# A hybrid diffusion layer with 16 experts: in experts 1 to 13 the next rows are turned later on VectorE and the ranking counts move behind the evacuations; one block of work is moved ahead in three other places

## The chip, the cores and the metric

The kernel runs on one core of one Trainium2 chip. The metric is the device time of one execution in microseconds (us); lower is better. The program is written by hand for each engine: TensorE (PE), VectorE (DVE), ScalarE (ACT), GpSimd (POOL) and SyncE (SP, which only issues DMA transfers). Each engine works through its own list in order, and semaphores tie the lists together.

## The reference, cut to what matters

One layer of a hybrid trunk, on 128 context tokens and 1024 latent tokens of width 1024. First a token mixer (a gated linear memory "mLSTM", a state space scan, and windowed attention, all from one projection), then a mixture of 16 experts in which every expert picks its tokens:

```python
def ec_moe(h, router_w, w1, w3, w2):
    xt = h.reshape(B * T, D)
    cap = EC_FACTOR * (B * T) // N_EXPERTS          # 128 latent, 16 context tokens
    aff = jax.nn.softmax((xt @ router_w).astype(jnp.float32), axis=-1)
    gate_vals, idx = lax.top_k(aff.T, cap)
    xe = xt[idx]
    hid = jax.nn.silu(jnp.einsum('ecd,edf->ecf', xe, w1)) * jnp.einsum('ecd,edf->ecf', xe, w3)
    ye = jnp.einsum('ecf,efd->ecd', hid, w2) * gate_vals[..., None]
    y = jnp.zeros_like(xt).at[idx.reshape(-1)].add(ye.reshape(-1, D).astype(xt.dtype))
```

Ahead of both halves each token row is normalised and modulated by six vectors `mod = silu(c) @ ada_w + ada_b`, whose products are cut into 24 slabs of 256 columns.

## The kernel before

All products are float32. The order of the work is written out by hand; two tables set where small pieces go.

**mLSTM stage.** 18 units (2 directions x 9 chunks of 128 tokens) run one after the other on PE: `m_scores(u + 1)`, `m_state(u)`, `m_values(u)`, `m_update(u)`. Between them stand blocks of the input projection ("T" blocks: 8 products of 128x384) and transposes ("X"), which the table `M_FILL` spreads over 36 slots. `M_FILL[0]` is called between `m_scores(0)` and `m_scores(1)`, and `m_scores(1)` waits for the weights of unit 0 (`mP`), which DVE makes from the scores of unit 0.

**Attention stage.** 27 units; `late_product(m)` for the last 16 slabs of `ada_w` stands behind the units of the list `MOD_UNITS`, and `late_pick(m)` one unit later.

**Expert stage.** For each of 16 experts PE makes `hidden(e)`: 8 blocks `fb`, each a product with w1 and one with w3 (8 matmuls each, 128x144), into PSUM banks 0/1 and 2/3; then `second(e)`: 8 blocks `db` of 8 matmuls with w2, by turns into bank 4 (even) and bank 5 (odd). I call the start of `hidden` N and the start of `second` T. ACT makes the silu of the w1 product, DVE multiplies it with the w3 product (the "mult", 8 per expert). ACT evacuates bank 4, DVE bank 5. Block `db` may only start when block `db - 2` is evacuated:

```python
pe.wait_ge(e_yA if db % 2 == 0 else e_yD, e * 4 + (db // 2 + 1))
```

In the same time the next expert is got ready:
- DVE `rank_begin(e+2)` and `rank_count(e+2, ...)` find each token's rank for expert e+2: 8 counts of 128x1024 in four pairs, and a cast of the ranks behind the second and the fourth pair, which sets `ranks_set`.
- POOL (`expert_rows`) then, strictly in order: four list scatters behind the first cast, four behind the second, the scatter of y of the expert before (four quarters, then a wait until they have landed), and the gather of the rows of expert e+1 (four quarters, `xq`).
- DVE `x_turned(e+1)` waits for that gather, turns the rows with four 32x32 stream transposes and sets `ex_full`. ACT and DVE (`x_evac`) each wait for `ex_full`, then scale half of the turned rows into `xeT`.
- On ACT `x_evac` stands ahead of the evacuation of `db` 0; in its list are 8 silus, `x_evac`, four evacuations, and the scaling of y.
- At the end of the expert DVE turns y (`yq`, 4 transposes) and scales it.

Experts 1 to 13 are a loop on ACT, DVE and POOL (the Fori of `expert(e, False)`); PE and SP are written out. Experts 0 and 14 turn the next rows on PE (`x_turn_latent`, 8 transposes into banks 6 and 7).

Of the kernel before, what the change touches and what calls it, by code (L numbers as in the profile page):

```python
# [22 lines left out]
KD = D // P  # L23
# [103 lines left out]
def hybrid_layer(nc, x_prompt, x_sample, cacheT_k, cache_v, state_c, state_n, state_sT, vec_rows, small_row, ada_w,  # L127
# [4 lines left out]
    groups, n_gate, n_early, n_first = plan_groups()  # L132
# [5 lines left out]
    def spread(first, last, slots):  # L138

        cost = [{"C": 0, "X": 4, "H": 3, "T": 52, "R": 34}[groups[n][0]] for n in range(first, last)]  # L140
        out, done, n = [], 0, first
        for t in range(slots):
            mine = []
            while n < last and (t == slots - 1 or done + cost[n - first] / 2 <= sum(cost) * (t + 1) / slots):
                mine.append(n)
                done += cost[n - first]
                n += 1
            out.append(mine)
        return out

    M_FILL = spread(n_early, n_first, 34) + [[], []]
    BRIDGE = [n_first, n_first + 1]
    base, S_FILL = spread(n_first + 2, len(groups), 33) + [[], [], []], []
    merged = groups[:n_first + 2]
# [46 lines left out]
    with ExitStack() as ctx:  # L201
# [236 lines left out]
        e_h1, e_h3, e_sil, e_hid = sem("e_h1_full"), sem("e_h3_full"), sem("e_silu_done"), sem("e_hidden_done")  # L438
        xgl_in, ex_full, ex_act, ex_dve = (sem(n) for n in ("e_gather_latent", "e_x_full", "e_x_act", "e_x_dve"))
# [75 lines left out]
            d, ch = UNITS[u]  # L515
            return (0 if ch == 0 else 2) + d

        MOD_UNITS = [1, 2, 5, 6, 8, 9, 11, 12, 13, 14, 17, 18, 19, 20, 22, 23]


        AU = [(hp, -1) for hp in range(HN // 2)] + [(hp, t) for hp in range(HN // 2) for t in range(NL)]
# [470 lines left out]
        def _(act):  # L992
# [401 lines left out]
            def silu_hidden(e, tiles={}):  # L1394

                for fb in range(KD):
                    act.wait_ge(e_h1, e * KD + (fb + 1))
                    act.wait_ge(e_hid, e * KD + (fb + 1))
                    nc.scalar.activation(sil[:, fb % 2, :], bk[fb % 2][:, 0:SLOTS], ACT.Silu).then_inc(e_sil, 1)  # L1399
                    for i in tiles.get(fb, ()):  # L1400
                        tile_square(i)

            def y_blocks(e, tiles=()):

                for db in range(0, KD, 2):
                    act.wait_ge(e_yt, e * KD + (db + 1))
                    nc.scalar.activation(yT[:, db, :], bk[4][:, 0:P], ACT.Copy, scale=modcol[:, 40 + db, 1:2])  # L1407
                    nc.scalar.activation(ycT[:, db, bass.ds(e, 1), :].rearrange("p a s -> p (a s)"), bk[4][:, P:SLOTS], ACT.Copy,
                                         scale=modcol[:, 40 + db, 0:1]).then_inc(e_yA, 1)
                    for i in tiles[db // 2:db // 2 + 1]:  # L1410
                        tile_square(i)

            def y_evac(e, rows=False):

                y_blocks(e)
                act.wait_ge(e_ty, e + 1)
                act.wait_ge(gcur_set, e + 1)
                if rows:
                    act.wait_ge(e_free, e + 1)
                    nc.scalar.activation(by_block(ye)[:, 0:4], block_rows(bk[6]), ACT.Copy, scale=gcur[:, 0:1]).then_inc(e_yeA, 1)  # L1420
                    return
                for a in range(2):
                    ins = nc.scalar.activation(yq[:, a, :], yq[:, a, :], ACT.Copy, scale=gcur[:, a:a + 1])
                ins.then_inc(e_yeA, 1)

            def one_expert(e, x_rows=False, y_rows=False):

                silu_hidden(e)
                act.wait_ge(ex_full, e + 2)
                act.wait_ge(e_h3, e * KD + KD)  # L1430
                x_evac(x_psum if x_rows else xturn)
                y_evac(e, y_rows)
# [26 lines left out]
        def _(pe):  # L1459
# [356 lines left out]
            a_scores(1)  # L1816
            pe.wait_ge(cache_in, 32)
            pe.wait_ge(sY, NU)
            for a in range(NA):
                if a + 2 < NA:  # L1820
                    a_scores(a + 2)
                if a >= 1:
                    a_values(a - 1)
                if a - 1 in MOD_UNITS:
                    late_pick(8 + MOD_UNITS.index(a - 1))
                a_turned(a)
                if a in LATE_UNITS:
                    y_late(LATE_UNITS.index(a))
                if a in MOD_UNITS:
                    late_product(8 + MOD_UNITS.index(a))  # L1830
                if a == MOD_UNITS[3] + 1:
                    pe.wait_ge(modT_done, 12)
                    nc.tensor.transpose(bk[7][0:16, 384:512], modcol[:, 16:24, :].rearrange("p a b -> p (a b)"), ident[:])\
                        .then_inc(g1_full, 1)
# [193 lines left out]

            for e in range(NE - 1):
                hidden(e)  # L2030
                if e in (0, NE - 2):
                    pe.wait_ge(xgl_in, fetched(e + 1))
                    pe.wait_ge(e_yeA, e + 1)
                    pe.wait_ge(e_yeD, e + 1)
                    x_turn_latent(0, KD)
                pe.wait_ge(e_hid, e * KD + (KD + 1))
                second(e)
                if e == 0:
                    pe.wait_ge(e_yA, e * 4 + 4)
                    pe.wait_ge(e_yD, e * 4 + 4)  # L2040
                    y_turned(e)
# [28 lines left out]
        def _(dve):  # L2070
# [609 lines left out]
            def expert(e, is_first, x_rows=False, is_last=False):  # L2680

                dve.wait_ge(e_yeA, e + 1)
                dve.wait_ge(e_yeD, e + 1)
                v.tensor_copy(gcur, lists[:, bass.ds(e * 8, 8)].rearrange("p (a w) -> p a w", w=2)[:, :, 1]).then_inc(gcur_set, 1)
                if is_first:
                    rank_begin(1)
                for fb in range(KD):
                    if is_first and fb < 3:
                        rank_count(1, ((0, 1, 2), (3, 4, 5), (6, 7))[fb])
                    dve.wait_ge(e_sil, e * KD + (fb + 1))  # L2690
                    dve.wait_ge(e_h3, e * KD + (fb + 1))
                    v.tensor_tensor(hid[:, fb, :], sil[:, fb % 2, :], bk[2 + fb % 2][:, 0:SLOTS], ALU.mult)\  # L2692
                        .then_inc(e_hid, 1)
                    if fb == KD - 2 and not (is_last or x_rows):
                        x_turned(e + 1)
                if is_last:
                    dve.wait_ge(vecs_in, 16 * 4)
                    tile_scales(1, 2)
                else:
                    dve.wait_ge(ex_full, e + 2)  # L2700
                    x_evac(e + 1, x_psum if x_rows else xturn)
                    rank_begin(e + 2)
                for db in range(1, KD, 2):
                    if not is_last:
                        rank_count(e + 2, (db - 1, db))
                    dve.wait_ge(e_yt, e * KD + (db + 1))
                    v.tensor_scalar(yT[:, db, :], bk[5][:, 0:P], modcol[:, 40 + db, 1:2], None, ALU.mult)
                    v.tensor_scalar(ycT[:, db, bass.ds(e, 1), :].rearrange("p a s -> p (a s)"), bk[5][:, P:SLOTS],
                                    modcol[:, 40 + db, 0:1], None, ALU.mult).then_inc(e_yD, 1)
                    if is_last and db < KD - 2:  # L2710
                        tile_scales(db + 2, db + 3)
                    if is_last and db == KD - 3:
                        dve.wait_ge(xgl_in, fetched(NE - 1) + 16)
                        dve.wait_ge(e_free, NE)
                        dve.wait_ge(gcur_set, NE)
                        last_rows(0)
                if is_last:
                    last_rows(1)
                    return
                dve.wait_ge(e_free, e + 1)  # L2720
                dve.wait_ge(gcur_set, e + 1)
                if is_first:
                    dve.wait_ge(e_ty, e + 1)
                    v.tensor_scalar(by_block(ye)[:, 4:KD], block_rows(bk[7]), gcur[:, 0:1], None, ALU.mult).then_inc(e_yeD, 1)
                    return
                dve.wait_ge(e_yA, e * 4 + 5)
                dve.wait_ge(e_yD, e * 4 + 5)
                for a in range(4):
                    ins = v.transpose(yq[:, a, :].rearrange("p (j k) -> p k j", k=KD), yT[:, :, 32 * a:32 * a + 32])
                ins.then_inc(e_ty, 1)  # L2730
                dve.wait_ge(e_ty, e + 1)
                for a in range(2, 4):
                    ins = v.tensor_scalar(yq[:, a, :], yq[:, a, :], gcur[:, a:a + 1], None, ALU.mult)
                ins.then_inc(e_yeD, 1)
# [71 lines left out]
```

## Time and profile before

| what | us |
|---|---|
| three runs | 1626.65, 1628.55, 1628.59 (median 1628.55) |
| the profiled execution, its time | 1628.24 |
| its span in the profile | 1626.5 |
| PE busy in it | 1579.8 |
| expert stage: first `hidden` starts, last block ends | 849.4, 1613.9 |

The profile follows one execution. "Busy" is the time in which an engine has an instruction in work; an idle time is put down to what ended it ("<-"). A float32 matmul shows as two records, so `second` of one expert (64 matmuls) has 128 records, and `hidden` 256. A line number is that of `kernel.py`.

### The profile page before, as it was taken

What the parts mean: (1) busy time and instruction counts of PE and PEld (TensorE: products, weight loads), DVE (VectorE), ACT (ScalarE), POOL (GpSimd) and SP (SyncE); (2) the same over time, 40 slices, a digit from 0 to 9 for tenths busy, and PEclk for the clock granted to TensorE, in tenths of its full rate; (3) what the DMA queues carried; (4) which work ended last, traced back from release to release, by engine and by line L of the source; (5) the groups of instructions that cost most, each with busy time, mean ns of one, the idle gap of its engine ahead of it and who ended that gap; (6) DMA issues with size and microseconds to landing.
All of it is one profiled execution on the core that took longest, in us unless ns stands there. A gap on an engine that the chain in (4) does not pass through costs nothing. (4 is left out here: it accounts for less than half of the span.)

```text
span 1626.5 us, 28425 instructions
## 1 busy us (share of the span) xinstructions
PE 1579.8 (97%) x11188; PEld 1377.2 (85%) x11188; DVE 714.6 (44%) x1867; ACT 387.3 (24%) x970; POOL 474.2 (29%) x556
## 2 busy tenths in 40 slices
PE   6999999999999899999988999999999999999997
PEld 5866876666668767788878999999999999999997
DVE  4001046776565844222363345444334454443344
ACT  5210113341222476411131111111111111111114
POOL 3000000015232643121202343433344343334432
PEclk9999999999999999999999999999999999999999
DMA  8302211132312476423259999999999999999985
GB/s 348 113 11 88 79 37 58 38 126 30 60 29 90 130 248 206 154 69 101 91 200 353 304 287 303 321 315 296 286 297 306 287 321 330 298 286 287 316 263 228
DMA packets 190733, 324.85 MB, mean 200 GB/s; under 512 B 36110, under 2 KB 76167, under 8 KB 185625
## 3 DMA queue, kind: packets, MB, share of 16 engines
q1 hardware_dynamic: 151017, 282.70, 50.7%
q0 software_dynamic: 15520, 17.45, 5.5%
q10 hardware_dynamic: 24080, 23.02, 5.1%
q8 instruction: 89, 1.46, 0.4%
q14 instruction: 27, 0.22, 0.0%
HBM read 294.42 MB, written 25.51 MB: 197 GB/s over the span
## 5 line engine op out<-in xcount | busy, mean ns | idle before, releaser
L1990 PE MATMUL psum<-arena 128*128 128x144 f32 x4096 | 504.8, 286 | 2.0 <-DVE arena L2632 1.7
L1990 PEld LDWEIGHTS psum<-arena 128*128 128x128 f32 x4096 | 502.9, 190 | 2.4 <-ACT arena L1367 1.9
L2002 PE MATMUL psum<-arena 128*128 128x144 f32 x2048 | 254.4, 286 | 0.0
L2002 PEld LDWEIGHTS psum<-arena 128*128 128x128 f32 x2048 | 252.8, 190 | 0.0
L1573 PE MATMUL psum<-arena 128*128 128x384 f32 x720 | 243.1, 493 | 0.0
L905 POOL DMA_INDIRECT expert_list<-gt x128 | 130.1, 1016 | 320.1 <-DVE gt L2662 286.5
L1573 PEld LDWEIGHTS psum<-arena 128*128 128x128 f32 x720 | 134.6, 191 | 90.2 <-issue 3.1
L2692 DVE TENSOR_TENSOR arena<-gt,psum 128x144 f32<-128x144 f32 x128 | 38.8, 303 | 360.3 <-PE psum L1990 310.3
L2514 DVE SCALAR_TENSOR_TENSOR arena<-arena,gt 128x1024 f32<-128x1024 f32 x128 | 159.1, 1280 | 0.5 <-DMA arena<-affinity_rows 0.5
L1576 PE MATMUL psum<-arena 128*128 128x256 f32 (+2 forms) x784 | 146.4, 346 | 0.0
L1576 PEld LDWEIGHTS psum<-arena 128*128 128x128 f32 x784 | 129.4, 190 | 15.5 <-issue 1.7
L1879 PE MATMUL psum<-arena 128*128 128x256 f32 x576 | 128.4, 381 | 0.7 <-DVE arena L2435 0.7
L1399 ACT ACTIVATE gt<-psum 128x144 f32<-128x144 f32 x128 | 37.0, 289 | 380.9 <-PE psum L1990 374.1
L1879 PEld LDWEIGHTS psum<-arena 128*128 128x128 f32 x576 | 107.9, 190 | 17.1 <-issue 2.1
L786 POOL TENSOR_TENSOR arena<-arena,gt 128x260 f32<-128x260 f32 x18 | 11.4, 635 | 307.6 <-DVE arena L2153 194.7
L955 POOL DMA_INDIRECT moe_latent<-arena,gt x56 | 88.2, 1576 | 24.2 <-issue 18.5
L1407 ACT ACTIVATE arena<-psum,modcol 128x128 f32<-128x128 f32 x64 | 23.5, 367 | 165.2 <-PE psum L2002 165.2
L939 POOL DMA_INDIRECT arena<-h_latent,gt x52 | 51.2, 984 | 23.8 <-issue 13.7
L827 POOL TENSOR_TENSOR arena<-Hst,gt 64x192 f32<-64x192 f32 x36 | 24.2, 673 | 112.0 <-DVE Hst L2351 110.6
L2417 DVE CUSTOM_DVE_ANT_0 gt<-psum,arena 128x512 f32<-128x512 f32 x48 | 31.3, 689 | 57.8 <-PE psum L1754 57.8
L888 POOL TENSOR_TENSOR arena<-arena 128x1024 f32<-128x1024 f32 x8 | 18.8, 2349 | 92.5 <-DVE arena L2471 92.5
L854 POOL TENSOR_TENSOR arena<-arena 128x384 f32<-128x384 f32 x30 | 30.0, 1017 | 47.2 <-DVE arena L2417 47.2
(379 smaller groups left out, 1632.1 us busy)
## 6 DMA issues: line engine op xcount, KB each, us to landing
arena<-in_exp_w SPq DMA_DIRECT2D x96, 2048.0 KB, 15.0
arena<-in_ada_w SPq DMA_DIRECT2D x24, 1024.0 KB, 7.0
arena<-in_w_in SPq DMA_DIRECT2D x11, 1024.0 KB, 4.9
arena<-in_x_sample SPq DMA_DIRECT2D x16, 512.0 KB, 4.4
arena<-affinity_rows SPq DMA_DIRECT2D x16, 512.0 KB
arena<-m_decay_rows ACTq DMA_DIRECT2D x36, 128.0 KB, 3.3
arena<-decay_rows ACTq DMA_DIRECT2D x24, 192.0 KB, 3.5
out<-arena SPq DMA_DIRECT2D x9, 512.0 KB, 2.6
```

Source lines behind the costliest of these rows:

```text
L905: pool.indirect_dma_start(out=list_d, out_offset=bass.IndirectOffsetOnAxis(ap=rank_i[:, c:c + 1].bitcast(U32), axis=0), in_=pair[:, c, :], ...
L939: pool.indirect_dma_start(out=xq[:, a, :], out_offset=None, in_=h2q_d, in_offset=bass.IndirectOffsetOnAxis(ap=icur[:, a:a + 1].bitcast(U32 ...
L955: pool.indirect_dma_start(out=accq_d, out_offset=bass.IndirectOffsetOnAxis(ap=icur[:, 4 + a:5 + a].bitcast(U32), axis=0), in_=yq[:, a, :], ...
L1399: nc.scalar.activation(sil[:, fb % 2, :], bk[fb % 2][:, 0:SLOTS], ACT.Silu).then_inc(e_sil, 1)
L1573: ins = mm(ps[0:cols, 0:384], ring[:, s % RING, k, col:col + cols], hT[:, k, i * 384:i * 384 + 384], start=(k == 0), stop=(k == KD - 1))
L1576: ins = mm(ps[:, 0:cols], hT[:, k, i * P:i * P + P], ring[:, s % RING, k, col:col + cols], start=(k == 0), stop=(k == KD - 1))
L1879: ins = mm(out, mixed(k, i), ring[:, (WOUT + j) % RING, k, :], start=(k == 0), stop=(k == KD - 1))
L1990: ins = mm(bank[:, 0:SLOTS], w[:, k, col], xeT[:, k, :], start=(k == 0), stop=(k == KD - 1))
L2002: ins = mm(bk[4 + db % 2][:, 0:SLOTS], wslot[4 + db // 4][:, k, (db % 4) * P:(db % 4) * P + P], hid[:, k, :], start=(k == 0), stop=(k == K ...
L2417: v.tensor_tensor_reduce(sc_sb[:, a % 3, e, :], ps, tab[:, table_of(a) % 2, e, :], -1.0, 3e38, ALU.add, ALU.min, accum_out=col).then_inc(a ...
L2514: return v.scalar_tensor_tensor(scratch, row, col, before[:, o:o + row.shape[1]], ALU.subtract, ALU.is_gt, accum_out=out)
L2692: v.tensor_tensor(hid[:, fb, :], sil[:, fb % 2, :], bk[2 + fb % 2][:, 0:SLOTS], ALU.mult)\
```

## The change

Five edits: (1) `M_FILL[0]` gets the first T block of the table, and the rest is spread over the slots again; (2) the first late product goes ahead of the unit loop; (3) in expert 0 PE does blocks 0 to 3 of `second` before it turns the rows of expert 1, ACT evacuates blocks 0 and 2 before its `x_evac`, and DVE blocks 1 and 3 before its own; (4) in experts 1 to 13 `x_turned(e+1)` moves behind the mult of `fb` 7 (before: behind that of `fb` 6); (5) in experts 1 to 14 each pair of counts stands behind the evacuation of its block (before: ahead of it). ACT's list in experts 1 to 13, and all of POOL's and SP's, stay.

```diff
-    M_FILL = spread(n_early, n_first, 34) + [[], []]
+    M_FILL = spread(n_early + 1, n_first, 34) + [[], []]
+    M_FILL[0] = [n_early] + M_FILL[0]
...
-        MOD_UNITS = [1, 2, 5, 6, 8, 9, 11, 12, 13, 14, 17, 18, 19, 20, 22, 23]
+        MOD_UNITS = [0, 2, 5, 6, 8, 9, 11, 12, 13, 14, 17, 18, 19, 20, 22, 23]
...
-                y_blocks(e)
+                y_blocks(e, blocks=range(KD // 2 if rows else 0, KD, 2))
...
                 silu_hidden(e)
+                if y_rows:
+                    y_blocks(e, blocks=range(0, KD // 2, 2))
...
+            late_product(8)
             for a in range(NA):
...
-                if a in MOD_UNITS:
+                if a in MOD_UNITS[1:]:
...
                 hidden(e)
+                if e == 0:
+                    pe.wait_ge(e_hid, e * KD + (KD + 1))
+                    second(e, range(0, KD // 2))
                 if e in (0, NE - 2):
...
-                    if fb == KD - 2 and not (is_last or x_rows):
+                    if fb == KD - 1 and not (is_last or x_rows):
                         x_turned(e + 1)
...
-                else:
+                elif not is_first:
                     dve.wait_ge(ex_full, e + 2)
                     x_evac(e + 1, x_psum if x_rows else xturn)
+                if not is_last:
                     rank_begin(e + 2)
                 for db in range(1, KD, 2):
-                    if not is_last:
+                    if is_first:
                         rank_count(e + 2, (db - 1, db))
                     dve.wait_ge(e_yt, e * KD + (db + 1))
                     v.tensor_scalar(yT[:, db, :], bk[5][:, 0:P], modcol[:, 40 + db, 1:2], None, ALU.mult)
...
+                    if not (is_first or is_last):
+                        rank_count(e + 2, (db - 1, db))
+                    if is_first and db == KD // 2 - 1:
+                        dve.wait_ge(ex_full, e + 2)
+                        x_evac(e + 1, x_psum)
```

DVE's list in the body of the loop, before, from the mult of `fb` 6 to the first scaling of the next rows (STREAM_TRANSPOSE x4 is `x_turned`, L2692 the mult):

```order
L2692 TENSOR_TENSOR arena<-gt,psum 128x144
L2622 ISA
L2625 STREAM_TRANSPOSE arena<-arena 128x8x32 x4
L2690 REGISTER_ALU
L2692 TENSOR_TENSOR arena<-gt,psum 128x144
L2700 REGISTER_ALU
L2630 TENSOR_SCALAR arena<-arena,gs,modcol 128x128 x4
```

The same place after; the transposes now stand behind the last mult (L2702), directly ahead of the scaling:

```order
L2702 TENSOR_TENSOR arena<-gt,psum 128x144
L2700 REGISTER_ALU
L2702 TENSOR_TENSOR arena<-gt,psum 128x144
L2632 ISA
L2635 STREAM_TRANSPOSE arena<-arena 128x8x32 x4
L2710 REGISTER_ALU
L2640 TENSOR_SCALAR arena<-arena,gs,modcol 128x128 x4
```

The end of the loop body on DVE before: the last two counts (L2514), the cast that releases POOL (L2662), the evacuation of `db` 7 (L2707, L2708), the transposes of y (L2729):

```order
L2514 SCALAR_TENSOR_TENSOR arena,gt<-arena,gt 128x1024
L2662 CAST gt<-gt 128x4
L2707 TENSOR_SCALAR arena<-psum,modcol 128x128
L2708 ISA
L2708 TENSOR_SCALAR arena<-psum,modcol 128x16
L2726 ISA
L2729 STREAM_TRANSPOSE arena<-arena 128x8x32 x4
```

And after; the evacuation is first, then the counts, the cast, and y:

```order
L2718 TENSOR_SCALAR arena<-psum,modcol 128x128
L2719 ISA
L2719 TENSOR_SCALAR arena<-psum,modcol 128x16
L2667 REGISTER_ALU
L2524 SCALAR_TENSOR_TENSOR arena,gt<-arena,gt 128x1024
L2667 REGISTER_ALU
L2524 SCALAR_TENSOR_TENSOR arena,gt<-arena,gt 128x1024
L2672 CAST gt<-gt 128x4
L2742 ISA
L2745 STREAM_TRANSPOSE arena<-arena 128x8x32 x4
```

PE's list after, from the first `hidden` (L1994) to that of expert 1; `second` (L2006) is cut in two around the 8 transposes of L1972, which stood ahead of all 64 before:

```order
L1994 MATMUL psum<-arena 128x144 x128
L2006 MATMUL psum<-arena 128x144 x32
L1972 MATMUL psum<-ident,arena 128x128 x8
L2006 MATMUL psum<-arena 128x144 x32
L2015 MATMUL psum<-ident,arena 128x128 x8
L1994 MATMUL psum<-arena 128x144 x128
```

## Rows read from the trace of the kernel before

**Rows 1.** Waits of PE, whole span: total us, times, longest us.
```profile
PE psum L1968 <- DMA arena<-h_latent,gt: 4.3, 1, 4.3
...
PE psum L1754 <- ACT gt L1268: 3.5, 1, 3.5
...
PE psum L1888 <- DVE gt L2508: 2.4, 1, 2.4
...
PE psum L1990 <- DVE arena L2632: 1.7, 1, 1.7
PE psum L1800 <- issue: 1.3, 1, 1.3
```
**Rows 2.** The chain that ended last: start us, us, what.
```profile
885.88 1.97 PE psum L1968 x8
887.85 16.28 PE psum L2002 x128
...
1124.68 15.68 PE psum L2002 x128
1140.37 31.36 PE psum L1990 x256
...
1548.13 0.88 PE psum L1968 x8
```
**Rows 3.** Windows of PE: length, busy, granted clock, DMA share, GB/s.
```profile
223.40:230.10 6.70, 6.70 (x27) 0.50 0.01 2
...
834.40:837.70 3.30, 3.30 (x10) 0.50 1.06 423
...
847.80:851.40 3.60, 1.96 (x16) 1.00 0.87 273
885.60:888.90 3.30, 3.02 (x14) 0.50 1.05 410
```
**Rows 4.** Timeline of DVE in experts 4 and 5: start us, us.
```profile
1092.38 0.17 DVE L2662 CAST gt<-gt 128x4 int32<-128x4 f32 x1
...
1099.23 0.30 DVE L2692 TENSOR_TENSOR arena<-gt,psum 128x144 f32<-128x144 f32 x1 [1.96 <-remote]
...
1121.85 2.22 DVE L2625 STREAM_TRANSPOSE arena<-arena 128x256 f32<-128x256 f32 x4 [0.68 <-DMA arena<-h_latent,gt]
1124.79 0.31 DVE L2692 TENSOR_TENSOR arena<-gt,psum 128x144 f32<-128x144 f32 x1 [0.72 <-PE psum L1990]
1125.02 1.11 DVE L2630 TENSOR_SCALAR arena<-arena,gs,modcol 128x128 f32<-128x128 f32 x4
...
1136.48 0.35 DVE L2707 TENSOR_SCALAR arena<-psum,modcol 128x128 f32<-128x128 f32 x1 [1.02 <-PE psum L2002]
...
1139.42 0.17 DVE L2662 CAST gt<-gt 128x4 int32<-128x4 f32 x1
```
**Rows 5.** Timeline of ACT in expert 7.
```profile
1219.39 1.65 ACT L1367 ACTIVATE arena<-arena,modcol,gs 128x128 f32<-128x128 f32 x4 [2.25 <-DVE arena L2625]
...
1221.19 0.26 ACT L1408 ACTIVATE arena<-psum,modcol 128x16 f32 x1
```
**Rows 6.** Timeline of POOL in expert 5.
```profile
1093.34 0.97 POOL L905 DMA_INDIRECT expert_list<-gt  x1 [2.73 <-DVE gt L2662]
...
1112.09 1.05 POOL L939 DMA_INDIRECT arena<-h_latent,gt  x1 [0.84 <-POOLq L933]
...
1115.98 0.95 POOL L939 DMA_INDIRECT arena<-h_latent,gt  x1 [0.30 <-issue]
```
**Rows 7.** Waits of all engines: DVE's wait for the gathered rows.
```profile
DVE arena L2625 <- DMA arena<-h_latent,gt: 16.3, 12, 2.5
```
**Rows 8.** Timeline of DVE: the turning in expert 13.
```profile
1499.95 2.22 DVE L2625 STREAM_TRANSPOSE arena<-arena 128x256 f32<-128x256 f32 x4 [2.45 <-DMA arena<-h_latent,gt]
```
**Rows 9.** Timeline of PE: unit 1's scores in the mLSTM stage.
```profile
222.71 0.72 PE L1617 MATMUL psum<-arena 64*128 64x128 f32 x8 [1.93 <-DVE arena L2269]
```
**Rows 10.** Timeline of PE: the first late product.
```profile
568.75 1.07 PE L1800 MATMUL psum<-arena,scol 128*32 128x256 f32 x16
```

More of the change, by code:

```diff
@@ L1401, in silu_hidden, with y_blocks @@
                         tile_square(i)
-            def y_blocks(e, tiles=()):
-                for db in range(0, KD, 2):
+            def y_blocks(e, tiles=(), blocks=range(0, KD, 2)):
+                for db in blocks:
                     act.wait_ge(e_yt, e * KD + (db + 1))
@@ L2035, in _ @@
                     x_turn_latent(0, KD)
-                pe.wait_ge(e_hid, e * KD + (KD + 1))
-                second(e)
+                if e == 0:
+                    second(e, range(KD // 2, KD))
+                else:
+                    pe.wait_ge(e_hid, e * KD + (KD + 1))
+                    second(e)
                 if e == 0:
```

## Prediction

> **What bounds the kernel now.** I read the table of the page first: PE is busy for 1579.8 of 1626.5 us. So nothing that another engine saves counts by itself; only PE's own gaps can be gained, and a new gap on PE is lost in full. The view of PE's waits lists them: 4.3 us in expert 0 for the gathered rows of expert 1, 3.5 at the start of attention, 2.4 in the router, 1.7 ahead of the first expert, 1.3 ahead of the second late product [rows 1]. In the chain that ended last the reader is to see the steady beat of the experts: 15.68 us of `second`, 31.36 of `hidden`, 47.04 together, so 0.245 us for a matmul and 1.96 for a block of 8 [rows 2]. In experts 1 to 13, where the largest part of the change lies, PE has no wait in the list at all: there the change can win nothing, and the question is what slack its moves use up.
>
> The windows show a second price of a gap. After the 4.3 us wait the granted clock is 0.50 for 3.3 us, that is 1.2 in place of 2.4 GHz; it is 0.50 as well after the 2.4 us wait (from 834.4) and for 6.7 us at the start of the mLSTM stage, but 1.00 around the 1.7 us wait at 849 [rows 1, 3]. What such a drop costs the chain shows: the 8 transposes take 1.97 us behind the wait and 0.88 in expert 14, the 128 records behind them 16.28 in place of 15.68 [rows 2]. That is 1.09 + 0.60 = 1.69 us.
>
> **Edit 3, expert 0: gain 6.0 us.** Blocks 0 to 3 of `second` need only the hidden values and their slot of w2; they cover 4 x 1.96 = 7.84 us, and the rows arrived 4.28 us after the last block of `hidden`. So the wait goes, and the drop with it: 4.28 + 1.69 = 5.97. Evacuations of both engines now stand ahead of their `x_evac`; between the transposes and the next `hidden` there are four more blocks, 7.8 us, against 1.65 us of `x_evac` on ACT [rows 5]. No new wait.
>
> **Edit 1, the mLSTM start: gain 5.2 us.** PE stands 1.93 us between the two scores, waiting for DVE's weights of unit 0 [rows 9], and then has 6.7 us at half clock [rows 3], which is 3.35 us of lost work. A T block of 8 products fills the gap; it is PE work that has to be done anyway. 1.93 + 3.35 = 5.3 us, of which I take 5.2. If the drop stays (the scores ahead of it are small), 1.9 is left. The other moves in that stage only shift blocks by a slot between units where PE does not wait; I cost them at nothing, since the fill of the neighbouring slot covers DVE and ACT; without it one unit's wait like the 1.93 would come back.
>
> **Edit 2, the attention start: gain 2.0 us.** The first late product takes 1.07 us [rows 10] and moves into the 3.5 us wait; the second then waits no longer for the results of the first, 1.3 us [rows 1]. Together 2.4; ACT gets two small evacuations ahead of its turned rows, for which I take 0.4 off. The three gains make 13.2 us.
>
> **Edits 4 and 5, experts 1 to 13, first cost: turning later.** Count from T. The last mult starts 0.11 us after T, and DVE is free 0.23 us after that [rows 2, 4]: turning can start at T + 0.34 at the earliest. It takes 2.22 [rows 4]. ACT's `x_evac` follows; from its start to the end of the evacuation of `db` 0, which stands behind it, is 1219.39 to 1221.19 + 0.26 = 2.06 us [rows 5]. With 0.12 us for two semaphores, bank 4 is free 2.22 + 2.06 + 0.12 = 4.40 us after turning starts. PE wants it for `db` 2 at T + 2 x 1.96 = T + 3.92. So a PE wait of start - T + 0.48 us opens in every expert, at least 0.34 + 0.48 = 0.82 us. Before, turning started some 2.2 us ahead of T and this wait could not occur. Behind ACT's `x_evac` queue its four evacuations, and behind PE's `db` 2 everything else. DVE's own evacuation of `db` 1 stands behind two small steps as well, but PE asks for it a block later, at T + 5.88 plus the wait: hidden.
>
> **Second cost: the casts come later, and with them the gather.** Where the counts of `db` 7 stood ahead of its evacuation, the cast began at N(next) - 0.95 (1139.42 against 1140.37) [rows 2, 4]. Now the evacuation comes first, about N + 0.03; from the start of an evacuation through two counts to the end of the cast is 1136.48 to 1139.59, 3.11 us [rows 4]. So the cast ends at N + 3.14 instead of N - 0.78: 3.92 us later. Queued behind it on POOL, with no slack between, are four list scatters, the scatter of y, its landing, and the gather: the list scatters start 0.79 us after the cast of 1092.38 ends, and the last gather is issued to 1116.93, 23.6 us later; DVE turns at 1121.85, 4.9 after that [rows 4, 6]. That this chain already ends last, the waits say: DVE waited for the gathered rows in 12 of the 13 experts, 16.3 us in all, 1.36 each [rows 7]. In expert 5 it waited 0.68 and started 2.83 us ahead of T [rows 2, 4]; so the mean start is 2.83 - (1.36 - 0.68) = 2.15 ahead of T, and the latest, in expert 13 with 2.45, is 2.83 - 1.77 = 1.06 ahead [rows 8]. Shifted by 3.92 the gather lands 1.77 us after T on the mean, later than T + 0.34. PE's wait becomes 1.77 + 0.48 = 2.25 us, in experts 2 to 13; expert 1, whose gather does not stand behind such a scatter, has 0.82. The wait doesn't feed on itself: the casts hang on N, and N on T plus the wait. Sum: 12 x 2.25 + 0.82 = 27.8 us.
>
> **Third cost: the clock.** Waits of 2.4 and 4.3 us were followed by a drop, one of 1.7 was not. The twelve waits run from 1.57 (expert 5: 3.92 - 2.83 + 0.48) to 3.34 (expert 13). I take 5 drops of 1.69, 8.5 us; the ends are none and all twelve, 20.3.
>
> **Is the first mult of the next expert late?** DVE now scales y 2.6 us later (the counts in front of it, less the end of its wait for the last evacuation). The first mult stood at 1099.23, which with N = 1140.37 - 47.04 is N + 5.9 [rows 2, 4]; PE needs its result for `fb` 2 at N + 7.84. Its wait is marked "remote", so the profile doesn't name the releaser. Either it hangs on N, and y's delay is hidden, or on DVE's own list, and PE waits 1 us there. In that case T moves 1 us later and the wait at `db` 2 gets 1 us shorter, since the gather hangs on N: the period is the same. I cost it at nothing.
>
> **Sum.** Against the profiled execution, 1628.24 us, which is 0.3 under the median of the runs: 1628.2 - 13.2 + 27.8 + 8.5 = 1651.3 us. About 0.2%, 3.3 us, is what a measurement can tell from no change here.
>
> **Bounds of the gather.** What isn't measured is how long y and the rows take to land at other times against the weight transfers. From the last issue to the turning it is 4.9 us now. A landing 1 us quicker makes 12 us less and nearly no drop (1651 - 12 - 5 = 1634); 1 us slower, if y's scatter now meets the weights, 12 us more and some 3 drops (1651 + 12 + 5 = 1668). This is the range.
>
> **Rivals.**
> *The gather catches up.* It now falls later between the weight transfers and lands so much quicker that DVE turns at once. Then only 0.82 x 13 = 10.7 us and no drops stand against 13.2 of gains: 1625.7, not slower. It decides when the rows land by T + 0.3, so when at least 1.5 us of the 3.92 are won back in every expert. For it: part of the landing is contention (DMA share 1.05 in the windows of this stage [rows 3]). Against: all 12 experts waited, with much the same landing, and the weights of a slot are issued at set times of PE's work. The page "DMA: Bandwidth & Descriptors" of the Trainium skill, section "Anatomy of one DMA", puts a transfer issued by GpSimd at about 2.0 us plus its bytes by 436 GB/s, an estimate of 2.3 us for a quarter of 128 KB. By it the landing would be 2.6 us quicker, and this rival would come true; the trace does not agree so far, it shows 4.9.
> *Every wait drops the clock*, and landing is slower by a little: 27.8 + 20.3 - 13.2 over 1628.2, 1663; with the landing 1 us slower 1675.
> *The early moves do nothing*: the fill waits for something else (its slab, or ACT), and the drops at both stage starts stay. Then the gains are 6.0 + 1.9 + 1 = 8.9, and the time is 1655.6. For it: the first window at the mLSTM start has small products either way.
> *The gains are larger*: the drop at the attention start goes too, 3.4 us, together with the first rival: 1622.3, faster.
>
> **Chances.** Forecast, within 1634 to 1668: 0.80. All clocks drop or slower landing, above it: 0.07. The gather catches up, 0.10, of which 0.04 with enough gain to be faster than 1625.0 and 0.06 within 0.2%. Between 1631.5 and 1634: 0.03. So faster 0.04, same 0.06, slower 0.90; the range leaves 0.07 above and 0.13 below. The early moves doing nothing lies inside it.
>
> **What would show it.** In the waits of PE: a new line `second` <- ACT (the evacuation of bank 4), 13 times, 0.8 in expert 1 and 1.5 to 3.4 in the others; the line L1968 <- DMA gone. In the chain: `second` at about 18 instead of 15.68 us, `hidden` unchanged. In DVE's timeline: turning starts T + 0.3 in expert 1 and T + 1 to T + 3 in the others, its wait still ended by the DMA; the last cast ends 3.1 us after N. On POOL the first of the last four list scatters at N + 3.9. Windows: no half clock at 223 to 230 and 885. Wrong it would be if turning starts at T + 0.3 in all experts (first rival), or if PE's wait stands at `fb` 2 and `db` 2 both with the period growing by their sum.

## The result, and the profile after

The changed kernel takes 1758.4 us (median of 4 runs, 1755.2 to 1760.7) against 1627.9 for the kernel before in the same comparison (4 runs, 1626.65 to 1628.59): ratio 1.0797, 95% interval 1.0781 to 1.0814. Slower, as forecast, but by 130 us, not by 23: the time is far outside 1634 to 1668. Of the 129.5 us between the two profiled spans, experts 1 to 13 take 135.1 more, expert 14 2.2 and expert 15 1.6 more; the work ahead of the experts takes 3.1 less and expert 0 6.2 less.

The waits of PE over the whole span (total us, times, longest us) show where; the lines answer to [rows 1].

```profile
PE psum L2006 <- ACT arena L1409: 103.5, 14, 9.7
...
PE psum L1576 <- ACT arena L1082: 3.9, 1, 3.9
...
PE psum L1892 <- DVE gt L2518: 2.4, 1, 2.4
PE psum L1757 <- ACT gt L1269: 2.3, 1, 2.3
PE psum L1972 <- DMA arena<-h_latent,gt: 2.0, 1, 2.0
```

The first line is the wait that was forecast, `second` behind ACT's evacuation of bank 4, at the engine and the block where it was forecast. But it is 103.5 us in place of 27.8. The second is new and was not foreseen. The 4.3 us wait of expert 0 is gone, and a like one has come up in expert 14.

The waits of the other engines, after, lead back to the cause. DVE waits 92.0 us for the gathered rows (16.3 in [rows 7]), and POOL 110.8 us for the scatter of y to land, 9.2 us each time. In the kernel before, POOL's wait was 51.0 us, 4.25 each time (first line).

```profile
POOL gt L917 <- DMA moe_latent<-arena,gt: 51.0, 12, 5.2
```
```profile
ACT arena L1368 <- DVE arena L2635: 147.3, 13, 13.1
...
POOL gt L918 <- DMA moe_latent<-arena,gt: 110.8, 12, 10.2
...
DVE arena L2635 <- DMA arena<-h_latent,gt: 92.0, 12, 8.9
```

One expert (4) in the timelines of the changed kernel. First POOL: the first list scatter behind the last cast, the last three quarters of y's scatter, the resumption once y has landed, the first and last quarter of the gather.

```profile
1066.00 0.97 POOL L906 DMA_INDIRECT expert_list<-gt  x1 [2.72 <-DVE gt L2672]
...
1074.22 1.57 POOL L956 DMA_INDIRECT moe_latent<-arena,gt  x1 [0.30 <-issue]
1076.10 1.55 POOL L956 DMA_INDIRECT moe_latent<-arena,gt  x1 [0.30 <-issue]
1077.95 1.54 POOL L956 DMA_INDIRECT moe_latent<-arena,gt  x1 [0.30 <-issue]
1088.15 0.19 POOL L918 COPY gt<-gt 128x4 f32 x1 [8.65 <-DMA moe_latent<-arena,gt]
...
1089.65 1.05 POOL L940 DMA_INDIRECT arena<-h_latent,gt  x1 [0.84 <-POOLq L934]
...
1093.56 0.95 POOL L940 DMA_INDIRECT arena<-h_latent,gt  x1 [0.30 <-issue]
```

SyncE issues the first weight slab of the next expert between the second and the third quarter of y:

```profile
1075.82 0.55 SPq L654 DMA_DIRECT2D arena<-in_exp_w  x1
```

In the kernel before, POOL's and SyncE's timelines show the same two steps of expert 5 the other way round: the last quarter is issued until 1106.83, and the first slab at 1107.08, a quarter of a microsecond behind it.

```profile
1105.29 1.54 POOL L955 DMA_INDIRECT moe_latent<-arena,gt  x1 [0.30 <-issue]
...
1110.58 0.19 POOL L917 COPY gt<-gt 128x4 f32 x1 [3.74 <-DMA moe_latent<-arena,gt]
```
```profile
1107.08 2.51 SPq L653 DMA_DIRECT2D arena<-in_exp_w  x2
```

And what follows on DVE, ACT and PE in the changed kernel. The rows come 6.70 us after the gather's last issue (1093.56 + 0.95 to 1101.21), DVE turns, ACT scales, then evacuates bank 4, and PE goes on 8.19 us late. T is 1093.26 here and N, 31.36 earlier, 1061.90, so turning starts at T + 8.0; the forecast was T + 1.8 on the mean.

```profile
1093.26 4.08 PE L2006 MATMUL psum<-arena 128*128 128x144 f32 x32
...
1101.21 2.18 DVE L2635 STREAM_TRANSPOSE arena<-arena 128x256 f32<-128x256 f32 x4 [7.37 <-DMA arena<-h_latent,gt]
1103.43 1.65 ACT L1368 ACTIVATE arena<-arena,modcol,gs 128x128 f32<-128x128 f32 x4 [11.63 <-DVE arena L2635]
...
1105.23 0.26 ACT L1409 ACTIVATE arena<-psum,modcol 128x16 f32 x1
...
1105.54 14.54 PE L2006 MATMUL psum<-arena 128*128 128x144 f32 x96 [8.19 <-ACT arena L1409]
```

Windows of the changed kernel (PE busy, PE weight load, DVE, ACT, POOL, then granted clock, DMA share, GB/s): while y lands the DMA engines are full; around the wait the clock is at its lower level.

```profile
1075.80:1087.40 11.60, 11.60 (x97) 11.60 (x97) 0.92 (x3) 0.87 (x3) 3.10 (x2) 1.00 1.05 277
...
984.40:994.60 10.20, 5.77 (x24) 5.77 (x25) 6.59 (x17) 2.59 (x8) 0.00 (x0) 0.50 0.44 171
...
1622.70:1632.80 10.10, 4.79 (x20) 4.79 (x21) 6.59 (x17) 2.59 (x8) 0.00 (x0) 0.50 0.61 238
```

The last two are the first and the last of twelve such stretches of some 10 us, one in each of experts 2 to 13. From one `hidden` to the next it is now 57.5 to 59.8 us, 58.2 on the mean, and not 47.04: about 8.5 of wait, and the rest, 2.7, goes with the half clock.

### The profile page after: what moved, and what is told of

Its sections match the earlier page's. It is cut to its first block and busy times, and to the rows that moved or that the text cites. A ratio compares the mean times of both kernels' runs of the same rounds, so it can differ in the third digit from the quotient of the medians.

```text
span 1756.0 us, 28439 instructions
## 1 busy us (share of the span) xinstructions
PE 1607.7 (92%) x11188; PEld 1402.7 (80%) x11188; DVE 716.6 (41%) x1867; ACT 384.1 (22%) x970; POOL 474.2 (27%) x556
## 5 line engine op out<-in xcount | busy, mean ns | idle before, releaser
L1994 PE MATMUL psum<-arena 128*128 128x144 f32 x4096 | 504.8, 286 | 1.7 <-DVE arena L2642 1.7
L1994 PEld LDWEIGHTS psum<-arena 128*128 128x128 f32 x4096 | 502.9, 190 | 2.2 <-ACT arena L1368 1.9
L2006 PE MATMUL psum<-arena 128*128 128x144 f32 x2048 | 286.7, 306 | 103.7 <-ACT arena L1409 103.5
L2006 PEld LDWEIGHTS psum<-arena 128*128 128x128 f32 x2048 | 281.9, 208 | 106.9 <-ACT arena L1409 106.5
L1576 PEld LDWEIGHTS psum<-arena 128*128 128x128 f32 x720 | 135.0, 192 | 94.5 <-ACT arena L1082 4.0
L2702 DVE TENSOR_TENSOR arena<-gt,psum 128x144 f32<-128x144 f32 x128 | 39.0, 304 | 366.5 <-PE psum L1994 280.3
L1579 PEld LDWEIGHTS psum<-arena 128*128 128x128 f32 x784 | 129.4, 190 | 15.5 <-issue 1.7
L1883 PEld LDWEIGHTS psum<-arena 128*128 128x128 f32 x576 | 107.9, 190 | 17.1 <-issue 2.1
L2635 DVE STREAM_TRANSPOSE arena<-arena 128x256 f32<-128x256 f32 x52 | 28.4, 603 | 92.0 <-DMA arena<-h_latent,gt 92.0
L2718 DVE TENSOR_SCALAR arena<-psum,modcol 128x128 f32<-128x128 f32 x64 | 22.4, 351 | 90.4 <-PE psum L2006 78.0
L940 POOL DMA_INDIRECT arena<-h_latent,gt x52 | 51.1, 983 | 23.8 <-issue 13.7
L1368 ACT ACTIVATE arena<-arena,modcol,gs 128x128 f32<-128x128 f32 x52 | 21.4, 482 | 147.3 <-DVE arena L2635 147.3
## 6 DMA issues: line engine op xcount, KB each, us to landing
arena<-in_exp_w SPq DMA_DIRECT2D x96, 2048.0 KB, 11.6
```

Source lines behind the costliest of these rows:

```text
L940: pool.indirect_dma_start(out=xq[:, a, :], out_offset=None, in_=h2q_d, in_offset=bass.IndirectOffsetOnAxis(ap=icur[:, a:a + 1].bitcast(U32 ...
L1576: ins = mm(ps[0:cols, 0:384], ring[:, s % RING, k, col:col + cols], hT[:, k, i * 384:i * 384 + 384], start=(k == 0), stop=(k == KD - 1))
L1579: ins = mm(ps[:, 0:cols], hT[:, k, i * P:i * P + P], ring[:, s % RING, k, col:col + cols], start=(k == 0), stop=(k == KD - 1))
L1883: ins = mm(out, mixed(k, i), ring[:, (WOUT + j) % RING, k, :], start=(k == 0), stop=(k == KD - 1))
L1994: ins = mm(bank[:, 0:SLOTS], w[:, k, col], xeT[:, k, :], start=(k == 0), stop=(k == KD - 1))
L2006: ins = mm(bk[4 + db % 2][:, 0:SLOTS], wslot[4 + db // 4][:, k, (db % 4) * P:(db % 4) * P + P], hid[:, k, :], start=(k == 0), stop=(k == K ...
```

## The experiments

Theory A is what these rows suggest: the later cast pushes y's scatter and the gather into the weight transfers, their landing gets longer, and the late rows hold ACT's list in front of bank 4. The rivals: B, the turning's new place is the cost by itself; C, the engines' lists are too long for the beat; D, the landing is late for a reason of its own, not the weights. Each kernel was compared with the kernel before on the same chip (median 1628.6, then 1628.9 us).

**Edit 5 undone, edit 4 undone, both undone.** The three kernels keep edits 1 to 3; the first piece is e1, the second e2, and e3 has both.

```diff
-                    if is_first:
+                    if not is_last:
                         rank_count(e + 2, (db - 1, db))
...
-                    if not (is_first or is_last):
-                        rank_count(e + 2, (db - 1, db))
```
```diff
-                    if fb == KD - 1 and not (is_last or x_rows):
+                    if fb == KD - 2 and not (is_last or x_rows):
```

> The changed kernel with edit 5 undone in experts 1 to 14 (each pair of counts ahead of the evacuation of its block, as before); edits 1 to 4 stay. Theory A (the later cast pushes the scatter of y and the gather into the weight transfers, and the late rows hold ACT's list): the cast is back at N - 0.8, the rows are back 2 us ahead of T, turning starts at T + 0.34 behind the last mult, PE waits 0.8 us at block 2 in 13 experts and the clock does not drop; 1628.2 - 9.4 (the measured gains of edits 1 to 3) + 10.7 = 1629.5 us. Theory B (the place of the turning behind the last mult is what costs 10.9 us in each expert): stays near 1750 us.

> The changed kernel with edit 4 undone (DVE turns the next rows behind the mult of block 6 again); edit 5 (counts behind the evacuations) stays. Theory A: the rows are as late as in the changed kernel, N + 39 to 40; DVE now stands at the turning with the last mult behind it, so PE waits for that mult in block 0 of second in place of block 2: rows at N + 39.3, turning 2.2, mult 0.2 against N + 33.1 give a wait of about 8.8 us and the same clock drops, 1755 to 1765 us. Theory B: the gain of undoing it is nearly all of the loss, about 1630 us.

> The changed kernel with edits 4 and 5 both undone: only the three early moves are left. Both theories: no PE wait in experts 1 to 13, 1628.2 - 9.4 = 1618.8 us. If it is above 1622, part of the loss sits in edits 1 to 3 and the account of the experts is too small.

Measured: 1636.4 us (ratio 1.0044, 1.0027 to 1.0062), 1753.3 (1.0764, 1.0745 to 1.0783), and 1618.55 (0.9933, 0.9916 to 0.9951). So B falls as the main cause: moving the turning alone costs 1636.4 - 1618.55 = 17.9 us, and beside the late casts 1758.4 - 1753.3 = 5.1 us. The late casts without it cost 1753.3 - 1618.55 = 134.8 us. The waits of PE, first e1, then e2, show that the late rows hold whatever stands behind the turning; in e2 that is the last mult, with the same 104 us:

```profile
PE psum L2006 <- ACT arena L1409: 10.0, 13, 0.8
```
```profile
PE psum L2006 <- DVE arena L2702: 104.8, 12, 9.7
```

e1 is 7 us above its forecast, since 0.82 us an expert was too small. The bank 4 wait, 0.77 us in the view of waits, holds up `second` by 1.04 in all (e5, below, has it alone, with a beat of 48.08 us in place of 47.04), and DVE, whose counts now stand ahead of its evacuation of block 1 and behind the late turning, holds block 3 for 0.36 more: 17.08 us for `second` in place of 15.68, in 13 experts 18.2.

**The same late casts, with less behind the turning.** In experts 1 to 13 ACT evacuates blocks 0, 2 and 4 and DVE blocks 1, 3 and 5 before they touch the next rows.

```diff
 # ACT
                 silu_hidden(e)
-                if y_rows:
-                    y_blocks(e, blocks=range(0, KD // 2, 2))
+                head = KD // 2 if y_rows else 0 if x_rows else KD - 2
+                y_blocks(e, blocks=range(0, head, 2))
                 act.wait_ge(ex_full, e + 2)
...
 # DVE, behind the evacuation of block db
+                    if db == KD - 3 and not (is_first or x_rows or is_last):
+                        x_turned(e + 1)
+                        dve.wait_ge(ex_full, e + 2)
+                        x_evac(e + 1, xturn)
```

> The changed kernel, with the casts as late as in it, but in experts 1 to 13 ACT evacuates blocks 0, 2 and 4 ahead of its scaling of the next rows, and DVE evacuates blocks 1, 3 and 5 ahead of turning and scaling them (its counts of block 5 behind that). Theory A: rows still land some 8 us behind T, but now only what stands behind block 5 waits for them: turning at T + 12.1, 2.2 us, ACT's scaling until T + 16.0 against the end of second at T + 15.7, so PE waits some 0.4 us an expert, no drop, period 47.5 in place of 58: 1619 to 1630 us. A rival, C (the landing of the rows hangs on PE's waits, or DVE has too much in its list for 47 us): the rows come later still than T + 12 and PE waits over 2 us an expert, above 1645 us.

Measured: 1643.1 us (1.0088, 1.0071 to 1.0105). POOL waits for y nearly as long as in the changed kernel (100.7 us in 12), the gather is issued as late (until N + 33.3 to 34.9, there N + 31.8 to 34.6), and still 115 of the 140 us are gone. Two short waits of `hidden` are left, 1.1 us an expert, for ACT's scaling and for DVE's mult, and no half clock in the stage (the waits of PE, whole span):

```profile
PE psum L1994 <- DVE arena L2702: 8.2, 13, 0.6
PE psum L1994 <- ACT arena L1368: 6.2, 13, 0.5
```

That is above the 1630 of theory A, as the delays to DVE's mult were not counted, and below the 1645 of C.

**The weights.** The changed kernel, but from expert 2 on the first two slabs, the next two, or all four of w1 and w3 bring an eighth of their bytes. The diff is that of e5; e6 has slabs 2 and 3 in the list, e7 all four.

```diff
-                sp.dma_start(wslot[q], one[:, :, 512 * half_q:512 * half_q + 512]).then_inc(w_in_slot[q], 16)
+                n = 1 if e > 1 and q in (0, 1) else KD
+                sp.dma_start(wslot[q][:, 0:n], one[:, 0:n, 512 * half_q:512 * half_q + 512]).then_inc(w_in_slot[q], 16)
```

> The changed kernel, but for experts 2 to 15 the first two weight slabs (first halves of w1 and w3, 2 MB each, issued at N + 13.9 and 15.9) bring only one eighth of their bytes; the rest of the slot keeps the weights of expert 1, so the output is not the reference's. The transfers keep their places and their order. Theory A (y's scatter is late because it meets these slabs): y lands about 3.3 us behind its last issue again, N + 21 in place of N + 26; the gather is issued by N + 28, still ahead of the third slab, and lands 4 to 6 us behind that, so turning starts at T + 1 to T + 3 in place of T + 8: the PE wait falls from 8.5 to 1.5 to 3.5 us, 1640 to 1680 us. Theory D (the landing of y has nothing to do with the weights, it is late because of the queue or its own additions): y still lands at N + 26 and the time stays within 10 us of 1758.

> The same with the third and fourth slab (second halves of w1 and w3, issued at N + 29.6 and 31.6) cut to an eighth in experts 2 to 15 (output not the reference's). Theory A: y stays late at N + 26, the gather (issued until N + 33) now meets no slab and lands 2.5 to 4 us behind its last issue, N + 36: PE's wait falls by 2 to 4 us an expert, 1705 to 1735 us. Theory D: 1758 within 10.

> Both pairs of slabs cut to an eighth in experts 2 to 15 (output not the reference's). Theory A: y at N + 21, gather issued by N + 28 and landed by N + 31.5, so DVE turns behind its last mult at T + 0.34 in most experts and PE waits 1.4 us an expert as in the kernel with edit 5 undone: 1635 to 1642 us, no drops. If it stays above 1660, something besides the slabs makes y or the rows late.

Measured, one run each: 1633.9, 1721.1 and 1635.5 us. D falls, and C with it, since all lists are those of the changed kernel and the beat is 48.08 us. With the first pair light, and nothing else touched, 124 of the 140 us are gone: POOL waits 4.5 us for y in place of 9.2 (the waits, e5), and turning starts right behind the last mult. That is below the 1640 to 1680 of theory A, which had the rows land 4 to 6 us behind the gather's last issue; they are there within 2.5 to 4.1.

```profile
POOL gt L919 <- DMA moe_latent<-arena,gt: 53.8, 12, 5.3
...
PE psum L2007 <- ACT arena L1410: 10.0, 13, 0.8
```

With the second pair light y stays late (111.5 us in 12, e6), and only the gather's share comes back, 37 us; in one expert its last quarter is issued until 1089.29, and the rows are there at 1091.75, 2.46 us later, in place of 6.70. POOL's and DVE's timeline of e6:

```profile
1088.33 0.96 POOL L941 DMA_INDIRECT arena<-h_latent,gt  x1 [0.30 <-issue]
```
```profile
1091.75 2.18 DVE L2636 STREAM_TRANSPOSE arena<-arena 128x256 f32<-128x256 f32 x4 [3.79 <-DMA arena<-h_latent,gt]
```

Over the twelve experts of e6 the rows come 1.9 to 3.1 us behind the last issue. Since the slabs are issued at set places of PE's work, y decides: on time, it lets the gather slip in between the two pairs; late, it sends the gather into the second pair. No run keeps the late cast and issues full slabs later, so what the order alone would give back isn't measured.

**Smaller shifts of the cast.** Edits 1 to 3, turning behind block 6 as before; behind the evacuation of block 7 stands only the last count and the cast (e8), or the cast alone (e12; `rank_cast` is the cast taken out of `rank_count`).

```diff
 # e8
-                        rank_count(e + 2, (db - 1, db))
+                        rank_count(e + 2, (db - 1, db) if is_first or db < KD - 1 else (db - 1,))
...
+                    if db == KD - 1 and not (is_first or is_last):
+                        rank_count(e + 2, (db,))
 # e12
+                    if late and not is_last:
+                        rank_cast(e + 2, db)
```

> Edits 1 to 3 with the casts as before but for one count: in experts 1 to 14 the very last count (tile 7) stands behind the evacuation of block 7, so the last cast ends at about N + 2.0 in place of N - 0.8, 2.8 us later (the changed kernel: 3.9); turning stands behind the mult of block 6 as before. Were the landing times those of before, the rows would come at N + 32, and PE would wait 1.5 us for the last mult: 1618.6 + 20 = 1638 us. Theory A: y's last quarters are issued at N + 16.5, behind the first slab at N + 13.9, so y and the gather land later by more than the shift: rows at N + 35 to 38, a PE wait of 4 to 8 us an expert with drops: 1680 to 1740 us.

> Edits 1 to 3, with all counts ahead of the evacuations as before, but in experts 1 to 14 the last cast alone stands behind the evacuation of block 7: it starts at N + 0.3 in place of N - 0.95, 1.3 us later. y's last quarter is then issued until N + 15.0, just behind the first slab at N + 13.9 (before: N + 13.7). A constant landing would bring the rows at N + 30.3 at the latest 31.6, and PE would not wait or under 1 us: 1618 to 1625 us. Theory A: y's last quarters meet the slab, y lands 2 to 6 us later in place of 1.3, the rows at N + 31 to 36, and PE waits 1 to 5 us an expert for the last mult: 1635 to 1700 us.

Measured: 1742.3 us (1.0685, 1.0651 to 1.0718), just above theory A's range, and 1664.35 (1.0221, 1.0205 to 1.0236). In the traces y's last issue ends at N + 13.7 in e3, 15.05 in e12, 16.4 in e8 and 17.6 in e2, so e12's shift is 1.4 us. With it POOL already waits 99.5 us for y in 12 experts, 8.3 each (waits of e12), against 50.2, 4.2 each, in e3 (first line):

```profile
POOL gt L918 <- DMA moe_latent<-arena,gt: 50.2, 12, 5.0
```
```profile
POOL gt L918 <- DMA moe_latent<-arena,gt: 99.5, 12, 10.4
...
PE psum L2006 <- DVE arena L2706: 35.4, 12, 8.0
```

| kernel | y's last issue later by | POOL's wait for y, mean | median us |
|---|---|---|---|
| edits 1 to 3 (e3) | 0 | 4.2 | 1618.6 |
| cast alone behind (e12) | 1.4 | 8.3 | 1664.4 |
| last count and cast (e8) | 2.7 | 8.5 | 1742.3 |
| both counts and cast (e2) | 3.9 | 9.2 | 1753.3 |

It is a step, not a slope: of the 5.0 us that the wait for y grows by at 3.9 us of shift, 4.1 are there at 1.4, where a slope would give 1.8. That e8 is so much slower than e12 is the gather's part. The third slab is issued at N + 29.6. In nine of e12's twelve experts the gather's last issue ends by N + 29.7 and the rows are there 2.2 to 3.9 us later; in the other three it ends at N + 30.5 to 31.8, and they come 5.9 to 7.1 us later. In e8 it ends behind N + 30.4 in all twelve, and they come 5.3 to 8.8 us later. y's last quarter goes out until 1011.45 in one expert of e12, behind the slab of 1010.30 in SyncE's timeline of e12.

```profile
1009.89 1.56 POOL L956 DMA_INDIRECT moe_latent<-arena,gt  x1 [0.30 <-issue]
```
```profile
1010.30 0.55 SPq L654 DMA_DIRECT2D arena<-in_exp_w  x1
```

**The early moves.** Where did edit 1's gain go? The kernel before with edits 2 and 3; the same with only the pull of one T block from slot 1 to `M_FILL[0]`; and the kernel before with edit 1.

```diff
 # e10, beside edits 2 and 3
     M_FILL = spread(n_early, n_first, 34) + [[], []]
+    for slot in M_FILL:
+        if n_early in slot:
+            slot.remove(n_early)
+    M_FILL[0] = [n_early] + M_FILL[0]
```

> The kernel before with edits 2 and 3 alone (first late product ahead of the attention units, blocks 0 to 3 of second ahead of the turn in expert 0). Theory E (edit 1 loses at its second place what it wins at its first: its table brings the first T block of the fifth conv tile one slot earlier, where ACT cannot evacuate it yet, and PE waits 3.9 us with 6.8 us of half clock behind it): the mLSTM stage, from the first score to the last update, is 134.4 us again in place of 135.9, so this is 1.0 to 1.6 us faster than edits 1 to 3 together: 1617 us. The prediction's own account (edit 1 wins 5.2 us): this is slower than edits 1 to 3 by 5 us, 1624 us.

> Edits 2 and 3, and of edit 1 only the pull: the first T block goes from slot 1 to M_FILL[0], and all others stay in their slots of before. Theory E: the gain at the start (1.9 us of wait and up to 3.4 of half clock) comes without the later wait, 2 to 5 us faster than edits 2 and 3 alone: 1612 to 1615 us, the line L1576 <- ACT L1082 gone. Rival: slot 1 is empty now and PE waits there for the results of unit 0 instead, so the gain is under 1 us: 1616 to 1618 us.

> The kernel before with edit 1 alone. Theory E: 1.0 to 1.6 us slower than before, 1630 us, with the 3.9 us wait for ACT's evacuation at 320 to 327 us and the half clock behind it. The prediction's account: 5.2 us faster, 1623 us.

Measured: 1618.9 us (0.9944, 0.9930 to 0.9957), 1614.2 (0.9922, 0.9908 to 0.9935), 1629.45 (1.0004, 0.9995 to 1.0013). Edit 1 is worth nothing, alone or beside the others (e9 was to be 1.0 to 1.6 us faster than e3 and is not), and the pull alone some 4.7 us by the medians; the two intervals against the kernel before still touch. In the changed kernel the start of the stage does what was forecast (PE's timeline), but a T block of the fifth conv tile, one slot earlier by the new table, stands before a bank that ACT has not evacuated yet, and the clock is at its lower level around the end of that wait (windows):

```profile
220.72 5.43 PE L1576 MATMUL psum<-arena 128*128 128x384 f32 x16
226.08 0.72 PE L1620 MATMUL psum<-arena 64*128 64x128 f32 x8
...
327.42 2.93 PE L1576 MATMUL psum<-arena 128*128 128x384 f32 x4 [3.87 <-ACT arena L1082]
```
```profile
325.60:332.40 6.80, 4.98 (x8) 2.86 (x9) 6.51 (x16) 2.49 (x4) 0.00 (x0) 0.50 0.15 39
```

In e10 that wait is not in the list, and the clock is 1.00 from 325 to 333 us. e10 is the fastest kernel of the study, 0.8% under the kernel before.

## Why the prediction was right in direction and wrong in size

- **Edit 3, 6.0 us: right.** From N of expert 0 to that of expert 1 the changed kernel takes 6.2 us less, and no new wait stands there.
- **Edit 1, 5.2 us: wrong; 0 measured (e11).** The gap at the start was filled and the half clock behind it went. The step that failed is "The other moves in that stage only shift blocks by a slot between units where PE does not wait; I cost them at nothing": 3.9 us of wait came up 100 us later, and with it 3.4 us lost at half clock (1.7 in the traces of e3 and e11).
- **Edit 2, 2.0 us: not apart from noise.** Edits 2 and 3 give 9.1 to 10.0 us against 8.0 forecast (from e9's medians 10.0, from its ratio 9.1); in the traces PE's waits at the attention start are 2.3 and 0.2 us in place of 3.5 and 1.3, so the mechanism fits. The half clock there (0.50 from 561.3 to 568.1 us in the kernel before) is gone in the changed kernel's trace (1.00) but there again in those of e3 and e9, which have edit 2 too; no run ties it to the edit.
- **First cost, 0.82 us an expert: mechanism right, size 1.04** (1.40 with the counts ahead, which the forecast did not need). e5 shows it with everything else out of the way: 13 waits, 10.0 us or 0.77 each, and a beat longer by 1.04.
- **Second cost, the cast 3.92 us later: right.** In expert 4 of the changed kernel the last four list scatters begin at 1066.00, N + 4.1 (forecast N + 3.9), and y's last issue ends at N + 17.59 in place of N + 13.67.
- **The step that failed is "Shifted by 3.92 the gather lands 1.77 us after T on the mean"**: it passes the shift on one for one, with both landings as they were (4.9 us from the last issue of the gather to the turning), and the range allowed 1 us either way. POOL's wait for y went from 51.0 / 12 = 4.25 to 9.23 us, that is 5.0 more, and the gather's from 4.9 to about 6.3. 2.25 + 5.0 + 1.4 is 8.65 us; the waits are 8.19 in expert 4 and (103.5 - 1.7) / 12 = 8.5 on the mean. The bounds text had named the cause ("if y's scatter now meets the weights") and priced it at 1 us, with no row for that price.
- **Third cost, 5 drops of 1.69: wrong with it.** Waits of 8 us all drop the clock: twelve stretches of some 10 us at the lower level. From the start of expert 1 to that of expert 14 the changed kernel takes 135 us more, of which 102 are the twelve waits; most of the other 33, 2.7 each, goes with the half clock.
- **"The wait doesn't feed on itself": right.** The beat is 59.8 us once, then 57.5 to 58.4 without a trend: in every expert y's last issue ends at N + 17.6 and the first slab is issued at N + 13.9.
- **The first mult, costed at nothing: right in its price.** Of the two accounts neither is borne out as it stood: the mult now follows directly on DVE's own list (at N + 6.7 in place of N + 5.9), but that is still ahead of N + 7.84, and PE does not wait at block 2 of `hidden`.
- **Not foreseen, small:** the late gather also reaches expert 14 (2.0 us, L1972), and expert 15, which ends 1.6 us later after its start.

The first rival, that the gather falls between the weight transfers, is what e5 makes true by force, and what nine of the twelve experts of e12 show with full slabs; but there y's landing had already cost more than that wins. Of the Trainium skill, page "DMA: Bandwidth & Descriptors", section "Anatomy of one DMA", the estimate of 2.3 us for a quarter of 128 KB was set aside in the prediction because 4.9 were measured; with the second pair light (e6) the rows come after 2.46 us (1.9 to 3.1), so this case agrees with the page's figure where little else is under way, and the measured 4.9 held the weights' share already. The same page, section "Queues, rings and completion order", says that each DMA engine goes round by turns between the queues that have work. No run here shows the order of the packets; what this case shows is that y and the slabs move side by side: in expert 4, from the first slab's issue until y had landed, the weights' queue moved 3.1 MB and POOL's queue 0.4 MB.

## What to carry to other kernels

A transfer's landing time belongs to its place against the other transfers, not to the transfer: before a chain is moved, write down for each of its DMAs what is issued just behind it, and by how much. Here y's scatter had 0.25 us to the next 2 MB, and 1.4 us of delay cost 46 us. And a list in which one late input stands ahead of the releases that the busiest engine needs turns a late transfer into its wait; the same late rows cost 115 us less where three evacuations went first.

## What the runs showed of the hardware that was not expected

- A small scatter whose last quarters go out at or behind the issue of two 2 MB slabs takes 8.3 to 9.2 us from its last issue in place of 4.2, nearly the same whether only the last of four quarters runs into the first slab (e12) or two are issued behind it (changed kernel). By then most of the two slabs has been moved (3.1 MB in the expert above).
- The median landing of a 2 MB slab is 11.6 us in the changed kernel and 15.0 in the kernel before. In e1, where y lands as before and the beat is 48.4 us, it is 13.1; how much of the rest comes from the longer beat and how much from the order is not shown.
- The granted clock differs between executions of one kernel. In the five runs of e10 it is 0.992 to 0.999 on the mean, and the time follows it, 1618.6 to 1610.3 us. The first scores of the mLSTM stage begin at 220.07 us in the changed kernel and at 218.21 in e10, though all PE work ahead of them is the same; half clock at 28 us, there in the first trace and absent in the second, goes with it. So a single drop of 1.7 us can't be credited to an edit from one profile.
